# Attention on one core: ScalarE's order, values in two pieces, and two places each for turned probabilities in PSUM and SBUF

## What is computed

```python
s_win = jnp.einsum("bnqhgd,bnkhd->bnhgqk", qb, kw).astype(jnp.float32) * scale   # window of 3 blocks
s_ctx = jnp.einsum("bnqhgd,bkhd->bnhgqk", qb, kc).astype(jnp.float32) * scale    # 2 blocks of context
m = jnp.maximum(jnp.maximum(s_win.max(-1, keepdims=True), s_ctx.max(-1, keepdims=True)), sk)
p_win = jnp.exp(s_win - m)
p_ctx = jnp.exp(s_ctx - m)
inv = 1.0 / (p_win.sum(-1, keepdims=True) + p_ctx.sum(-1, keepdims=True) + jnp.exp(sk - m))
o = (jnp.einsum("bnhgqk,bnkhd->bnqhgd", p_win * inv, vw)
     + jnp.einsum("bnhgqk,bkhd->bnqhgd", p_ctx * inv, vc))
```

## Time and profile before

| what | value |
|---|---|
| median of 3 runs | 2914.42 us (2913.82 to 2914.52) |
| the profiled execution's own time | 2915.66 us |
| its span | 2913.70 us |
| mean granted clock of TensorE | 0.981 of full speed |
| TensorE matmul, busy | 2770.2 us (95%) |
| TensorE weight load, busy | 2478.7 us (85%) |
| VectorE, busy | 2066.9 us (71%) |
| ScalarE, busy | 1280.3 us (44%) |
| GpSimd, busy | 132.5 us (5%) |
| the attention, from the first scores to the last output copy | 1717.96 to 2030.94 us |

### The profile page before, as it was taken

The page is one execution under the profiler, slowest core; times in us unless marked ns, Lnnn a source line. Parts: engine busy times, 40 slices in busy tenths (PEclk is TensorE's granted clock), DMA queues, the critical chain, the costliest instruction groups (busy, mean ns, idle before and its releaser), DMA issues. The chain is left out here.

```text
span 2913.7 us, 45331 instructions
## 1 busy us (share of the span) xinstructions
PE 2770.2 (95%) x17546; PEld 2478.7 (85%) x17546; DVE 2066.9 (71%) x2901; ACT 1280.3 (44%) x1906; POOL 132.5 (5%) x177
## 2 busy tenths in 40 slices
PE   6999788999999999999999989998999999999997
PEld 5988687999999989999997767776989989778785
DVE  4999998988966476655758677665576558684565
ACT  4232244443446353333443568776453334443333
POOL 0000000000000000000000013333000000000000
PEclk9999789999999999999999999999999999999998
DMA  7556311223222222232223210000223232333332
GB/s 299 193 198 224 104 51 34 80 88 95 81 84 68 73 58 90 77 94 91 76 80 94 80 58 1 2 1 9 87 80 92 90 101 88 95 112 103 101 94 86
DMA packets 66520, 263.15 MB, mean 90 GB/s; under 512 B 6960, under 2 KB 7216, under 8 KB 60080
## 3 DMA queue, kind: packets, MB, share of 16 engines
q1 hardware_dynamic: 58368, 213.17, 23.6%
q0 software_dynamic: 5760, 41.95, 4.1%
q10 hardware_dynamic: 2224, 5.69, 0.6%
HBM read 256.58 MB, written 4.19 MB: 89 GB/s over the span
## 5 line engine op out<-in xcount | busy, mean ns | idle before, releaser
L1750 PE MATMUL PS<-a_hi,w_hi 128*128 128x322 f32 (+7 forms) x3584 | 916.3, 324 | 41.1 <-ACT a_hi L544 21.5
L1750 PE MATMUL PS<-a_lo,w_hi 128*128 128x322 f32 (+7 forms) x3584 | 890.2, 319 | 7.2 <-DVE a_lo L1087 6.9
L1750 PE MATMUL PS<-a_hi,w_lo 128*128 128x322 f32 (+7 forms) x3584 | 897.0, 319 | 0.0
L1750 PEld LDWEIGHTS PS<-a_hi,w_hi 128*128 128x128 f32 x3584 | 610.4, 191 | 99.2 <-issue 36.9
L1750 PEld LDWEIGHTS PS<-a_hi,w_lo 128*128 128x128 f32 x3584 | 611.8, 191 | 28.1 <-issue 4.6
L1750 PEld LDWEIGHTS PS<-a_lo,w_hi 128*128 128x128 f32 x3584 | 606.7, 191 | 32.6 <-DVE a_lo L1087 8.4
L1003 DVE TENSOR_TENSOR w_lo<-raw,w_hi 128x1024 fp32r<-128x1024 f32 (+2 forms) x380 | 444.9, 1171 | 186.6 <-ACT w_hi L497 183.0
L497 ACT ACTIVATE w_hi<-raw 128x1024 fp32r<-128x1024 f32 (+2 forms) x380 | 386.0, 1016 | 0.7 <-DMA raw<-wstream 0.6
L1750 PE MATMUL PS<-z_hi,w_hi 128*128 128x320 f32 (+1 forms) x1056 | 300.9, 339 | 8.1 <-ACT z_hi L748 5.7
L1750 PE MATMUL PS<-z_lo,w_hi 128*128 128x320 f32 (+1 forms) x1056 | 299.1, 337 | 0.8 <-DVE z_lo L1446 0.8
L1750 PE MATMUL PS<-z_hi,w_lo 128*128 128x320 f32 (+1 forms) x1056 | 298.1, 336 | 0.0
(11 more groups left out here) (251 smaller groups left out, 3206.4 us busy)
## 6 DMA issues: line engine op xcount, KB each, us to landing
raw<-wstream SPq DMA_DIRECT2D x380, 512.0 KB, 3.6
ada_slot<-adastream POOLq DMA_DIRECT2D x40, 1024.0 KB, 5.1
ada_first<-adastream SPq DMA_DIRECT2D x4, 2048.0 KB, 20.3
h<-xT SPq DMA_DIRECT2D x1, 2640.0 KB, 15.2
h<-xT ACTq DMA_DIRECT2D x1, 2480.0 KB, 13.3
out<-h ACTq DMA_DIRECT2D x1, 2048.0 KB, 9.3
out<-h SPq DMA_DIRECT2D x4, 512.0 KB, 2.7
rope_sb<-rope ACTq DMA_DIRECT2D x1, 1024.0 KB, 4.9
```

Of the source, the lines that this page charges most:

```text
L1750: last = MM(PS[:, 2 * j + m, 0:n], wt[:, j, k, :], mv[:, k, m * n:(m + 1) * n], start=start, stop=stop)
```

## The change

What it does, piece by piece:

- **Order on ScalarE.** In step n the exponential of head n and the cuts now come first, the copy of head n - 5 last.
- **Probabilities.** One ring of six heads (RING) takes the place of two buffers of four; an exponential waits for the transposes of six heads ago. GpSimd's scaling follows in its addresses.
- **Turned probabilities.** `pT` gets a second buffer, by the parity of the group; a copy waits for the values of two groups ago.
- **Transposes in PSUM.** Banks 4 to 6 are one row of 12 tiles. Even heads take the first tiles, odd heads the last ones. With 5 tiles each, bank 5 is shared by the fifth tile of an even head and the first of an odd one. This tile, the edge tile, is left out by `turn` and issued by `turn_last` one step later, behind the scores of that step. `turn` waits for the copy of two heads ago, `turn_last` for the copy of the head before. With 4 tiles there is no edge tile.
- **Values.** Each group's product is issued in a piece of three tiles (in the fourth step of a group, two groups later) and a piece of the remaining one or two (two steps on). It always writes bank 7, and waits for the output copy of the group before.
- **Output copy on VectorE.** It now comes in the second step of a group, behind the maximum of that head and ahead of the cut.
- **TensorE's order in step n:** scores of head n, edge tile of head n - 6, a piece of values, transposes of head n - 5.

```diff
@@ ScalarE @@
                     for n in range(N_HEADS + LAG):
                         g, hh, m = n // QPK, n % QPK, n - LAG
-                        if m >= 0:
...
-                            if above_zero(m // QPK):
-                                act.wait_ge(pv_done, m // QPK)
...
                         if n < N_HEADS:
                             w = len(attn_keys(g // 4)[0]) * BLK
                             act.wait_ge(neg_max, n + 1)
-                            if above_zero(n - 7):
-                                act.wait_ge(turned, n - 7)
+                            if above_zero(n - RING + 1):
+                                act.wait_ge(turned, n - RING + 1)
...
                             for c in range(cuts_by(n - 1), cuts_by(n)):
                                 cut(c)
+                        if m >= 0:
+                            nk = len(attn_keys(m // 16)[0])
+                            act.wait_ge(turned, m + 1)
+                            if above_zero(m // QPK - 1):
+                                act.wait_ge(pv_done, m // QPK - 1)
...
+                            at_pt = turn_at(m, 0, nk)
+                            A(pT[m // QPK % 2][:, 0:nk, m % QPK * BLK:(m % QPK + 1) * BLK],
+                              PS[:, 4:7, :].rearrange("p a b -> p (a b)")[:, at_pt:at_pt + nk * BLK].rearrange("p (a b) -> p a b", b=BLK),
+                              ACT.Copy).then_inc(pT_ready, 1)
@@ VectorE @@
-                    for n in range(N_HEADS + LAG + 2):
-                        g, hh, g_out = n // QPK, n % QPK, (n - LAG - QPK - 1) // QPK
-                        if g_out >= 0 and (n - LAG - 1) % QPK == 0:
...
+                    for n in range(N_HEADS + 10):
+                        g, hh, g_out = n // QPK, n % QPK, n // QPK - 3
...
+                        if g_out >= 0 and hh == 1:
+                            dve.wait_ge(pv_done, g_out + 1)
+                            nc.vector.tensor_copy(o_tiles_of(g_out), PS[:, 7, 0:2 * BLK].rearrange("p (a b) -> p a b", b=BLK)
+                                                  ).then_inc(o_stored, 1)
@@ TensorE and its helpers @@
+        def turn_at(m, t, nk):
+
+            return (t if m % 2 == 0 else 12 - nk + t) * BLK
+
+        def turn_edge(m, nk):
+
+            return 5 if nk == 4 else 4 if m % 2 == 0 else 0
...
                     def turn(m):
 
                         nk = len(attn_keys(m // 16)[0])
                         pe.wait_ge(prob_scaled, m + 1)
-                        if above_zero(m):
-                            pe.wait_ge(pT_ready, m)
+                        if above_zero(m - 1):
+                            pe.wait_ge(pT_ready, m - 1)
                         for t in range(nk):
...
+                            if t != turn_edge(m, nk):
+                                last = turn_tile(m, t, nk)
+                        if turn_edge(m, nk) == 5:
+                            last.then_inc(turned, 1)
+
+                    def turn_last(m):
+
+                        nk = len(attn_keys(m // 16)[0])
+                        if turn_edge(m, nk) < 5:
+                            if above_zero(m):
+                                pe.wait_ge(pT_ready, m)
+                            turn_tile(m, turn_edge(m, nk), nk).then_inc(turned, 1)
...
-                    scores(0)
-                    for n in range(N_HEADS + LAG + 1):
+                    for n in range(N_HEADS + 10):
                         m = n - LAG
-                        if m >= QPK and m % QPK == 0:
-                            values(m // QPK - 1)
+                        if n < N_HEADS:
+                            scores(n)
+                        if 1 <= m <= N_HEADS:
+                            turn_last(m - 1)
+                        if n >= 11 and n % QPK == 3 and n // QPK - 2 < N_GROUPS:
+                            values(n // QPK - 2, 0, 3)
+                        if n >= 13 and n % QPK == 1:
+                            values(n // QPK - 3, 3, 5)
                         if 0 <= m < N_HEADS:
                             turn(m)
-                        if n + 1 < N_HEADS:
-                            scores(n + 1)
```

More of the change, by code:

```diff
@@ L45 @@
 LAG = 5
+RING = 6
 AHEAD = 7
@@ L225, in backbone @@
         qs_lo = sb("qs_lo", [P, NQ, BLK], F32R, rX + 8192)
-        prob = [sb(f"prob{j}", [P, QPK, 5 * BLK], F32, rX + 16384 + 10240 * j) for j in range(2)]
+        prob = sb("prob", [P, RING, 5 * BLK], F32, rX + 16384)
+        rPT = rX + 16384 + RING * 2560
+        assert rPT + 10240 <= rX + 42240
         rB, rQ, rO, rR = rX + 42240, rX + 110976, rX + 94592, rX + 127360
@@ L237, in backbone @@
         rope_sb = sb("rope_sb", [P, 2, LAT], F32, rR)
-        pT = sb("pT", [P, 5, QPK * BLK], F32, rR)
+        pT = [sb(f"pT{j}", [P, 5, QPK * BLK], F32, at_pt) for j, at_pt in enumerate((rR, rPT))]
         wide = {"zA": zA, "zB": zB, "T": T, "y4": sb("y4", [P, KT, 516], F32, rB),
@@ L479, in _ @@
                     for hh in range(QPK):
-                        pr = prob[g % 2][:, hh, 0:w]
+                        pr = prob[:, (QPK * g + hh) % RING, 0:w]
                         nc.gpsimd.tensor_scalar(pr, pr, soft[:, 4, g % 2, hh:hh + 1], 1.0, ALU.mult,
@@ L2013, in scores, with turn_tile @@
                         last.then_inc(scored, 1)
+                    def turn_tile(m, t, nk):
+                        at_t = turn_at(m, t, nk)
+                        return nc.tensor.transpose(PS[:, 4 + at_t // 512, at_t % 512:at_t % 512 + BLK],
+                                                   prob[:, m % RING, t * BLK:(t + 1) * BLK], ident)
                     def turn(m):
@@ L2024, in turn @@
-                        last.then_inc(turned, 1)
-                    def values(g):
+                            if t != turn_edge(m, nk):
[8 more added lines that the diff above has]
+                            turn_tile(m, turn_edge(m, nk), nk).then_inc(turned, 1)
@@ L2028, in values @@
+                    def values(g, first, end):
                         kv = g % 4
                         tiles, _ = attn_keys(g // 4)
[L2030 to L2034, removed]
-                            heads = pT[:, t, :].rearrange("p (a c q) -> p c a q", c=2, q=BLK)
+                        if first == 0:
+                            pe.wait_ge(pT_ready, 4 * g + 4)
+                            pe.wait_ge(v_stored, x["v"])
+                            if above_zero(g):
+                                pe.wait_ge(o_stored, g)
+                        for t, tile in list(enumerate(tiles))[first:end]:
+                            heads = pT[g % 2][:, t, :].rearrange("p (a c q) -> p c a q", c=2, q=BLK)
@@ L2036, in values @@
                             for c in range(2):
-                                last = MM(PS[64 * c:64 * c + 64, 6 + g % 2, 0:2 * BLK].rearrange("p (a q) -> p a q", q=BLK),
+                                last = MM(PS[64 * c:64 * c + 64, 7, 0:2 * BLK].rearrange("p (a q) -> p a q", q=BLK),
                                           v_sb[:, tile, kv * HD:(kv + 1) * HD], heads[:, c],
                                           start=(t == 0), stop=(t == len(tiles) - 1), tile_position=(0, 64 * c))
-                        last.then_inc(pv_done, 1)
+                        if end == 5:
+                            last.then_inc(pv_done, 1)
```

16 lines of the change are left out of this document (3 added, 13 removed).

## The result

The changed kernel took 2871.64 us (median of 4 runs, 2871.00 to 2872.49), the kernel before 2914.12 us beside it: a ratio of 0.9854, with a 95% interval from 0.9837 to 0.9871. It is 42.5 us faster; 33.5 us had been forecast, so 9 us more came than the sum gave, inside the range of 2865 to 2900.

A forecast was written before the change was run, and what follows sets the result against it. TensorE and ScalarE bind by turns; with the waits gone TensorE bounds at 8.81 us a group instead of 9.79. Gains of 21.6 + 4.6 + 4.3 + 3.0 = 33.5 us give 2881 us, 80% range 2865 to 2900.

The forecast's parts named there:

- the scores of a head: TensorE's scores for one head, read from the trace as 1.06 us and counted four times a group.
- (1): ScalarE: the exponential goes ahead of the copy and no longer waits for a transpose; priced at nothing.
- (2): TensorE: values in pieces of three and two tiles, 1.45 and 1.02 us, 2.47 for 2.31, +0.16 a group.
- (3): Transposes in two PSUM places wait for the copy of two heads ago; edge tiles add 0.05 us per bound and hand-over.
- (4): Two pT buffers: a copy waits for the values of two groups ago; priced at nothing.
- (5): One output bank, copied by VectorE at a group's second head behind the maximum: next to no wait.
- (6): Round-trip walk: GpSimd's first scaling starts about 2.7 us, takes 0.90; transposes want it at 3.76, a few hundredths after.
- A: Rival, 12%: TensorE's pieces overlap more, ScalarE is left as the bound at 8.1 us a group; 2865 us.
- B: Rival, 20%: a wait, at GpSimd, edge tile or VectorE, replaces the removed one, 0.6 us a group; 2898 us.
- C: Rival, 4%: TensorE's changes between kinds of work drain the array, 0.38 us each, 11.1 us a group; 2931 us.
- D: Rival, 2%: short waits bring the granted clock down to 1.2 GHz for parts of the stretch; 2920 us.
- E: Rival, 2%: the change doesn't do what it says, ScalarE's order hangs on transposes as often as before; 2914 us.

The follow-up runs named there:

- e4: The kernel before with only ScalarE's order changed, exponential and cuts ahead of the copy: 2983.21 us, ratio 1.0237 to the kernel before.
- e5: The changed kernel with the values pieces turned round, two tiles first and the rest behind: 2871.15 us, ratio 0.9850 to the kernel before.
- e3: The changed kernel with all transposes in one place of PSUM again and no edge tile: 2915.18 us, ratio 1.0003 to the kernel before.
- e2: The changed kernel with each group's values again in one piece, at the group's second head: 2895.18 us, ratio 0.9937 to the kernel before.
- e1: The changed kernel with ScalarE's old order, copy ahead of the exponential: 2959.35 us, ratio 1.0155 to the kernel before.
- e10: The changed kernel with values pieces of two tiles then three, and ScalarE's exponential of the sinks behind the copy: 2873.93 us, ratio 0.9857.

## Why the prediction was right, and where its sum was off

**The mechanism held.** ScalarE's pause ahead of the copies went from 47.7 to 1.4 us, the long step of 3.74 us went, TensorE's queue became the bound, and the clock stayed at 1.00. The steps are 1.72, 2.36, 2.08 and 2.31 us, three of them inside the "2.0 to 2.6" that was to be seen and one 0.3 below it. The windows outside the middle were met within about 0.6 us each, in part by luck. Groups 1 to 5 took 8.5, 6.9, 7.4, 8.1 and 8.5 us against 8.3, 7.1, 7.1, 8.1 and 8.8, errors that cancel. Of the last groups the first took 7.5 against 8.6, and the next two 7.1 and 6.9 against 6.7 each. The gain of the tail holds 1.6 us of the clock.

**The term that was mis-sized** is the scores of a head: "1800.41 to 1801.47, 1.06 us". They cost 0.89. That stretch of the earlier trace rows ended with the change from scores to values, and 0.17 us of it were this change, which happens once a group in the kernel before and was counted four times. The changed kernel shows 0.89 from scores to transposes and from scores to the edge tile. That is 4 x 0.17 = 0.68 us too much. On the other side the edge tile with the change behind it costs 0.26 instead of 0.10 + 0.05, twice (0.22 too little: the upper bound of 0.16 for the hand-over was the right one, not the 0.05 taken), and the two-tile piece has GpSimd's 0.12. 8.81 - 0.68 + 0.22 + 0.12 = 8.47, against 8.45 as the mean of the window and 8.47 inside it. The 0.36 us a group that are left over are the whole surplus of the middle, 22 x 0.36 = 7.9 us of 9.

**Step by step.** (1) The exponential ahead of the copy, priced at nothing: true in company; alone it costs 2.4% (e4). The prediction said that what is queued behind the copy's wait is now only the next exponential, and did not say what waits for the copy: the next transposes, as long as they have one place. (2) The pieces: three tiles 1.45, two tiles 1.14 against 1.45 and 1.02. The hand-over of 0.16 us in each piece is there (e5, 1.01 for two tiles), so that the row was right, and not the time that the prediction worked out by the Trainium skill (TensorE: Matmul & The Clock Gate, Part 2), by which the second piece would cost nothing. (3) The second place: no transposes wait for a copy in the middle. It turned out to be the part without which the rest is worth nothing (e3). (4) The second pT buffer cannot be taken away alone in this order of the values, and was not tried: by the loops the first copy of a group would wait for values that stand behind transposes, and these would wait for copies. (5) The output copy: no wait worth a row in the middle. (6) The margins of the walk, "a few hundredths" at GpSimd: it came 0.12 us late. The walk took a quarter of 3.61 us, 0.90, for the first of the four scalings, which takes 1.03. And TensorE with its shorter scores asks for it sooner, 3.58 us after S0 (1848.36) and not 3.76.

**The rivals.** A (ScalarE's pace at 8.1 us) did not come, though the time came near it: TensorE is busy for 99% of the middle. B (a wait in place of the one removed) came at GpSimd, with 0.12 instead of 0.6 us. C (0.38 us at each hand-over) did not come: the change from scores to transposes costs 0.02. D did not come in the changed kernel. Nor did E: no exponential waits for a transpose, and ScalarE's idle time ahead of the copies is 1.4 us. e3 has the time that E gave, but by another way, since there TensorE waits for the copies.

## What to carry to other kernels

When two engines bind by turns, add up each one's queue from starts of instructions that follow the same kind of neighbour, and count the change from one kind of work to another where it happens, not in every instance. A block of work that another engine can't work through costs by its length as well as by its sum: 2.47 us in two pieces beat 2.31 us in one by 0.9 us a group (e2). And a reordering and a buffer can be worth nothing or less than nothing one by one and most of the gain together, so an ablation of one part says what the part is worth in company, not alone.

## What the runs showed that had not been expected

**The clock and the idle time.** In e4 the granted clock was 0.92 on the average over heads 24 to 111, in twelve separate drops to 1.2 GHz. In e1, whose groups are as long (11.81 us), it stayed at 1.00. Over the whole window TensorE seems as busy in e4 (207.24 of 267.84 us, 77%) as in e1 (198.39 of 259.87 us, 76%), but the two can't be compared so, since the same matmuls count longer at 1.2 GHz. In three groups of e4 at a full clock and three of e1 TensorE is busy for 73% and 77%:

```profile
1770.80:2030.67 259.87, 198.39 (x1578) 148.82 (x1576) 159.43 (x353) 171.11 (x374) 74.12 (x89) 1.00 0.00 1
...
1880.28:1915.72 35.44, 25.98 (x218) 21.18 (x217) 19.98 (x49) 23.30 (x51) 10.56 (x12) 1.00 0.00 1
...
1865.51:1901.03 35.52, 27.19 (x220) 20.41 (x216) 21.78 (x48) 23.34 (x51) 10.15 (x13) 1.00 0.01 1
```

The first row is e1's 22 groups, the second e4, the third e1 again. The longest pause of the matmuls differs too, 1.7 us in e4 and 1.4 us in e1. Which of the two brought the clock down in e4 is not shown.

**A wait that moves.** Four rearrangements each took away or shortened a wait of 0.10 to 0.12 us that the trace names, and each time a wait at another engine gave back half of it or all of it (e5: 0.14 for 0.12, e10: 0.05 for 0.10). A pause that a trace shows is worth its length only if no other engine is nearly as late.
